# One more projection tile computed between the DeltaNet products, and the attention's mask product in rounded float32

## The chip, the cores and the metric

The kernel runs on one core of a Trainium2 chip. The metric is the time of one execution on the device, in microseconds (us). Before the change the median of three runs is 2902.16 us (2899.98 to 2906.4).

## The reference, cut to what matters

A two-layer decoder trunk over T = 1040 tokens (16 meta tokens, 1024 of input), model width 1024. Layer 0 has one input projection that feeds 4 gated-DeltaNet heads and 4 stick-breaking attention heads:

```python
proj = u @ w_in                      # 28 tiles of 128 columns, and the gates
q_a, k_a, v_a = silu(causal_depthwise_conv(qkv_a, conv_w))      # tiles 0 to 11; z_a: tiles 12 to 15
o_a = gated_delta_rule_chunked(q_a, k_a, v_a, g, beta)          # sequential over chunks
# stick-breaking attention, tiles q 16-19, k 20-23, v 24-27, per block of 128 queries:
z = einsum("bqhd,bkhd->bhqk", qb, k) * head_dim ** -0.5
causal = key_pos < query_pos                                    # strictly
log_w = log_sigmoid(z) + (sum_of_log_1m_after_key)
w = where(causal, exp(log_w), 0);  out = w @ v
```

Then an output projection, a SwiGLU feed-forward layer, an S5 state-space mixer with a GLU, and a second feed-forward layer. Nothing of these later stages is touched.

## The kernel before, in words

**Matrix products.** Large products are done in a split form. Every weight tile (slab, 128x1024) is loaded by SP's queue into `stage`, and POOL splits it into a rounded high part `w_hi` and a rest `w_lo` (type fp32r, "the rounded form"). `gemm` (L720 to L723) then issues three fp32r matmuls: high by high, high by low, low by high. A tile of the input projection is 3 column cuts of the tokens (352, 344, 344) by 8 slices of the inner dimension by 3 matmuls, so 72 matmuls. One slice of one cut, 3 matmuls, is called a *step*. Products outside `gemm` are plain f32, which shows as two MATMUL instructions for each product.

**Input projection.** `FIRST_FILLED` is 20. A loop of five iterations of four tiles each (L891) computes tiles 0 to 19. It writes PSUM banks in a ring of six: a tile in slot j uses banks (3j+c) mod 6, so tile 18 uses banks 0 to 2 and tile 19 banks 3 to 5. ACT moves each group out of its bank (`conv_tiles`, `plain_tiles` at L1475) and stores each tile to the DRAM tensor `proj` (L1451). Between tiles 17 and 18, ACT issues thirteen small stores of S5 tables (L1507 to L1516). Then PE transposes the gates' rows (L898), and `in_proj_steps(0, 24)` computes tile 20 in one piece into banks 0, 1 and 2, each group after the wait at L913, which asks that the bank's former group has been moved out.

**DeltaNet.** Nine blocks of 128 tokens (n = 0 to 8; the first is 16 tokens). Each block inverts a triangular matrix in up to six levels. A level is a product p (`dn_level_p`, L996 and L991), a copy by ACT (L1622), a product up (`dn_level_up`, L1017, L1021, L1025, L1013), and a subtraction and transposition by DVE (L2399, L2401). Behind or between them stand the products of the previous block's output (`dn_ks` L1034, `dn_vn` L1041, `dn_o` L1051 and L1052, `dn_kdv` L1059, `dn_o_turn` L1064) and of the next block's preparation. After each p and each up there is a *gap*. `fill(gap)` (L1077) puts two steps of the remaining projection tiles there, from gap 1 on. With seven tiles left (168 steps) gaps 1 to 84 are filled. Gap 84 is behind the first p of block 8, so the last 11 gaps, 85 to 95, are empty. All filled tiles except the first use one bank, `fill_bank`. ACT moves a finished group out at L1554 and stores a finished tile at L1558.

After block 8's levels come its own output products, called the tail below: `dn_ks(8)`, which waits for DVE's gated output of block 7 (L2440), then `dn_vn`, `dn_o`, `dn_kdv`, `dn_o_turn`. ACT, in the same stretch, waits for the stores of all 28 tiles and for block 7's gated output, issues the loads of attention heads 0 and 1 (`load_head`, L1705), and goes on to `dn_vn_sb(8)` (L1627).

**Attention.** 36 rounds (4 heads by 9 query blocks, `g`). PE transposes round g's weights (L1157), computes the scores of round g+2 (L1142), and multiplies round g's weights by the values (L1170). Where a score chunk crosses the diagonal, a mask product follows (L1145): the identity, 128x128, by a 128-column matrix of zeros and -1e30, added into the scores' bank. There are 11 of them for each head, 44 in all. Values are transposed at L1126.

## Time and profile before

| what | value |
|---|---|
| median of three runs | 2902.16 us (2899.98 to 2906.4) |
| the profiled execution's own time | 2906.43 us |
| its span | 2904.6 us |
| PE busy | 2763.2 us, 95% |
| PE weight load | 2631.2 us, 91% |
| DVE, ACT, POOL busy | 42%, 21%, 33% |
| mean granted clock of PE | 0.971 |
| input projection, after the gates | 60.4 to 302.4 us of the span |
| DeltaNet | 302.4 to 601.0 us |
| attention | 601.0 to about 741 us |

A duration of a matmul in the timeline reaches beyond the next one's start, since they overlap; what one costs in a stream is the distance between starts. The clock column is the granted TensorE clock as a share of 2.4 GHz: 1.00 or 0.50 (1.2 GHz), or a mean where it changes inside a window.

### The profile page before, as it was taken

Reading aid. Unit: us, or ns where it says so; the run is one execution under the profiler, and the core shown is the slowest. Engines: PE = TensorE matmul, PEld = TensorE weight load, DVE = VectorE, ACT = ScalarE, POOL = GpSimd, SP = SyncE. Lnnn points to the kernel's source line nnn. Section 1 sums busy time; section 2 is a strip of 40 time slices with the busy share of each in tenths; the row PEclk is TensorE's granted clock in tenths of the full one; section 3 lists DMA queues with packets and bytes.
Section 4 is the critical chain, followed back from the end, with each engine's and each line's share of the span. In section 5 each row is a group of like instructions: output and inputs, shape, how many; then the busy total and the mean of one; then the engine's idle time right before and its main releaser. Section 6 shows DMA issues by size and latency. Waiting matters only on the chain.

```text
span 2904.6 us, 45080 instructions
## 1 busy us (share of the span) xinstructions
PE 2763.2 (95%) x18337; PEld 2631.2 (91%) x18337; DVE 1229.3 (42%) x2118; ACT 616.3 (21%) x1079; POOL 969.0 (33%) x390
## 2 busy tenths in 40 slices
PE   8999899989999999999999977799999999999996
PEld 7999688867889999999999866699989999999996
DVE  4655565556053444444432535520443222222234
ACT  4221333346241000000000331320420000000012
POOL 4544111000343444444343313134424444434430
PEclk7999999989999999999999988899999999999998
DMA  4236312110231222222222238642221111111112
GB/s 139 88 104 127 92 60 78 34 67 23 84 103 56 79 82 84 87 81 81 81 82 82 77 102 231 207 126 59 95 95 44 43 51 51 43 43 43 44 30 78
DMA packets 156979, 236.48 MB, mean 81 GB/s; under 512 B 57664, under 2 KB 120384, under 8 KB 153664
## 3 DMA queue, kind: packets, MB, share of 16 engines
q1 hardware_dynamic: 52400, 137.11, 15.3%
q10 hardware_dynamic: 104464, 97.71, 11.1%
q8 instruction: 87, 1.43, 0.2%
q14 instruction: 28, 0.23, 0.0%
HBM read 174.89 MB, written 64.09 MB: 82 GB/s over the span
## 4 chain that ended last, share of the span: by engine, by line
PE 37%; issue 36%; POOL 14%; DMA 6%; DVE 3%; ACT 2%; ACTq 1%; POOLq 0%; SPq 0%; DVEq 0%
POOL w_hi L694 9%; PE psum L721 8%; PE psum L722 8%; PE psum L723 8%; POOL w_lo L697 5%; DMA stage<-wstream 4%; PE psum L781 2%; PE psum L1170 2%; PE psum L1142 1%; PE psum L996 1%; PE psum L1250 1%; DMA area<-s 1%; PE psum L1157 1%; PE psum L1017 1%; DVE area L2085 1%
## 5 line engine op out<-in xcount | busy, mean ns | idle before, releaser
L721 PE MATMUL psum<-x_hi,w_hi 128*128 128x344 f32 (+3 forms) x3600 | 1178.0, 327 | 29.0 <-DVE x_lo L2109 23.3
L722 PE MATMUL psum<-x_lo,w_hi 128*128 128x344 f32 (+3 forms) x3600 | 1160.8, 322 | 0.0
L723 PE MATMUL psum<-x_hi,w_lo 128*128 128x344 f32 (+3 forms) x3600 | 1159.0, 322 | 0.0
L694 POOL TENSOR_TENSOR w_hi<-stage,const 128x1024 fp32r<-128x1024 f32 x193 | 485.0, 2513 | 1836.6 <-PE psum L723 1807.2
L721 PEld LDWEIGHTS psum<-x_hi,w_hi 128*128 128x128 f32 x3600 | 687.6, 191 | 41.2 <-DVE x_lo L2109 21.6
L722 PEld LDWEIGHTS psum<-x_lo,w_hi 128*128 128x128 f32 x3600 | 687.6, 191 | 3.5 <-issue 1.7
L723 PEld LDWEIGHTS psum<-x_hi,w_lo 128*128 128x128 f32 x3600 | 686.8, 191 | 0.0
L697 POOL TENSOR_TENSOR w_lo<-stage,w_hi 128x1024 fp32r<-128x1024 f32 x193 | 488.2, 2530 | 15.1
L721 PE MATMUL psum<-act_hi,w_hi 128*128 128x344 f32 (+2 forms) x1056 | 343.6, 325 | 19.8 <-DVE area L2580 15.2
L2567 DVE TENSOR_TENSOR area<-area,psum 128x344 f32<-128x344 f32 (+2 forms) x132 | 67.7, 513 | 656.0 <-ACT area L1828 655.8
L723 PE MATMUL psum<-act_hi,w_lo 128*128 128x344 f32 (+2 forms) x1056 | 338.5, 321 | 0.0
L722 PE MATMUL psum<-act_lo,w_hi 128*128 128x344 f32 (+2 forms) x1056 | 337.6, 320 | 0.0
L2580 DVE TENSOR_TENSOR area<-area,psum 128x344 f32<-128x344 f32 (+2 forms) x480 | 243.2, 512 | 187.2 <-PE psum L723 184.8
L1828 ACT ACTIVATE area<-psum 128x344 f32<-128x344 f32 (+2 forms) x132 | 60.5, 458 | 1229.4 <-PE psum L723 1229.3
L721 PEld LDWEIGHTS psum<-act_hi,w_hi 128*128 128x128 f32 x1056 | 199.5, 189 | 24.8 <-DVE area L2580 19.3
L722 PEld LDWEIGHTS psum<-act_lo,w_hi 128*128 128x128 f32 x1056 | 201.4, 191 | 0.2
L723 PEld LDWEIGHTS psum<-act_hi,w_lo 128*128 128x128 f32 x1056 | 199.5, 189 | 0.0
L2176 DVE TENSOR_TENSOR area<-area 128x512 f32<-128x512 f32 (+7 forms) x282 | 164.5, 631 | 46.0 <-PE psum L1270 25.3
L2570 DVE TENSOR_TENSOR act_lo<-area,act_hi 128x344 fp32r<-128x344 f32 (+2 forms) x132 | 104.6, 792 | 77.9 <-ACT act_hi L1832 77.9
L781 PE MATMUL psum<-area,const 128*128 128x344 f32 (+2 forms) x384 | 117.1, 459 | 16.0 <-ACT area L1375 14.1
L781 PEld LDWEIGHTS psum<-area,const 128*128 128x128 f32 x384 | 72.7, 192 | 52.1 <-issue 14.0
L2085 DVE SCALAR_TENSOR_TENSOR area<-area,small,psum 128x344 f32<-128x344 f32 (+2 forms) x96 | 47.4, 566 | 105.8 <-ACT psum L1386 105.8
(226 smaller groups left out, 2053.3 us busy)
## 6 DMA issues: line engine op xcount, KB each, us to landing
stage<-wstream SPq DMA_DIRECT2D x193, 512.0 KB, 3.6
s_set<-area ACTq DMA_DIRECT2D x8, 1860.0 KB, 7.8
area<-s SPq DMA_DIRECT2D x8, 1348.0 KB, 9.2
proj<-area ACTq DMA_DIRECT2D x20, 520.0 KB, 2.7
area<-proj ACTq DMA_DIRECT2D x36, 256.0 KB, 4.1
resid<-area ACTq DMA_DIRECT2D x6, 1376.0 KB, 6.1
area<-resid ACTq DMA_DIRECT2D x6, 1376.0 KB, 8.4
area<-s SPq DMA_DIRECT2D x8, 1024.0 KB, 9.2
```

Source lines behind the costliest of these rows:

```text
L694: pool.tensor_tensor(per_block(w_hi[:, slot, :]), src, ones_block, ALU.mult).then_inc(high_split, 1)
L697: pool.tensor_tensor(per_block(w_lo[:, slot, :]), src, per_block(w_hi[:, slot, :]).bitcast(F32), ALU.subtract).then_inc(split_done, 1)
L721: mm(out[:, 0:n], w_hi[:, slot, wk], hi[:, xk, a:a + n], start=first, stop=False)
L722: mm(out[:, 0:n], w_hi[:, slot, wk], lo[:, xk, a:a + n], start=False, stop=False)
L723: return mm(out[:, 0:n], w_lo[:, slot, wk], hi[:, xk, a:a + n], start=False, stop=last)
L781: last = mm(sums[:, 0:n], ones, sq[k // 4][:, k % 4, 0:n], start=(k == 0), stop=(k == KT - 1))
L1828: A(gate[st % 2][:, 0:n], bank[2 * (st % 2)][:, 0:n], ACT.Silu).then_inc(silu_done, 1)
L2085: last = V.scalar_tensor_tensor(out=acc[:, k, a:a + n], in0=acc[:, k, a:a + n], scalar=small[:, at:at + 1], in1=rr, op0=mul, op1=mul)
L2176: tt = lambda o, a, b, op: ch(V.tensor_tensor(o, a, b, op))
L2567: V.tensor_tensor(f[st % 2][:, 0:n], gate[st % 2][:, 0:n], bank[2 * (st % 2) + 1][:, 0:n], mul).then_inc(act_f32, 1)
L2570: V.tensor_tensor(act_lo[:, st % 2, a:a + n], f[st % 2][:, 0:n], act_hi[:, st % 2, a:a + n].bitcast(F32), sub).then_inc(act_ready, 1)
L2580: last = V.tensor_copy(o, src) if first else V.tensor_tensor(o, o, src, add)
```

## The change

`FIRST_FILLED` becomes 19. The loop runs four iterations, tiles 16, 17 and 18 follow it unrolled, and tile 19, the scaled query tile of head 3, is the first filled one: it is computed in one piece by `in_proj_steps(0, 24)` into banks 0, 1 and 2, which tile 18 used just before. Eight tiles are then left for the gaps (192 steps), so gaps 1 to 95 are filled and the last two steps stand in front of the tail. ACT evacuates the last group there, scales tile 19 in `filled_evac`, and asks for the last tiles' stores only before it loads head 2. The mask product takes both operands from `w_hi`, as fp32r, in a part of slot 5 that is free there; DVE writes them with one more copy.

```diff
-FIRST_FILLED = 20
+FIRST_FILLED = 19
...
+        mask_weights, mask_values = (w_hi[:, 5, 512 + P * i:512 + P * i + P] for i in range(2))
...
             with pe.Fori(0, FIRST_FILLED // 4) as i:
                 tile_groups("in_proj", i, 6)
+            tile_groups("in_proj", FIRST_FILLED // 4, 6, count=FIRST_FILLED % 4)
...
-                        pe.wait_ge(group_free, g + 1 if tile == 0 else 6 + g)
+                        pe.wait_ge(group_free, g + 4 if tile == 0 else 6 + g)
...
             o = BLOCKS - 1
+            in_proj_steps((N_PROJ - FIRST_FILLED) * 3 * KT - FILL_STEPS, FILL_STEPS)
             dn_ks(o)
...
-                        last = mm(z[0:nq, d - a:m], ident[:, 0:nq], sv["neg"][:, d - q0:a + m - q0], start=False, stop=True)
+                        last = mm(z[0:nq, d - a:m], mask_weights[:, 0:nq], mask_values[:, d - q0:a + m - q0], start=False, stop=True)
...
-            plain_tiles(SQ + 2, ACT.Copy, HD ** -0.5)
+            plain_tiles(SQ + 2, ACT.Copy, HD ** -0.5, 1)
...
             def load_head(hd):
+                if hd == 2:
+                    for i in range(2):
+                        act.wait_ge(proj_stored[i], 16 * (1 + N_PROJ // 2))
...
+            filled_evac(3 * (N_PROJ - FIRST_FILLED) - 1)
             for i in range(2):
-                act.wait_ge(proj_stored[i], 16 * (1 + N_PROJ // 2))
+                act.wait_ge(proj_stored[i], 16 * (1 + SV // 2 + 1))
             act.wait_ge(dn["o_gated"], BLOCKS - 1)
             load_head(0)
             load_head(1)
...
-            V.tensor_scalar(sb_views(carve)["neg"], incl, -1e30, None, mul).then_inc(sk["neg"], 1)
+            V.tensor_copy(mask_weights, ident)
+            V.tensor_scalar(mask_values, incl, -1e30, None, mul).then_inc(sk["neg"], 1)
```

## Rows read from the trace of the kernel before

**Rows 1.** The page, busy time and share of the span of each engine.
```profile
PE 2763.2 (95%) x18337; PEld 2631.2 (91%) x18337; DVE 1229.3 (42%) x2118; ACT 616.3 (21%) x1079; POOL 969.0 (33%) x390
```

**Rows 2.** Timeline of ACT, end of the projection: start, length, instruction, [idle before <-releaser].
```profile
289.57 0.63 ACTq L1516 DMA_DIRECT2D s_tab<-area  x1
290.30 1.16 ACT L1475 ACTIVATE area<-psum 128x352 f32<-128x352 f32 x3 [23.32 <-PE psum L723]
```

**Rows 3.** Timeline of PE, from the end of the projection loop to DeltaNet's first product.
```profile
289.24 0.77 PE L898 MATMUL psum<-const,area 64*128 64x64 f32 x9
290.91 0.40 PE L721 MATMUL psum<-x_hi,w_hi 128*128 128x352 f32 x1 [0.90 <-ACT area L1475]
...
303.79 1.10 PE L935 MATMUL psum<-area,const 128*128 128x512 f32 x2 [1.27 <-ACT area L1579]
```

**Rows 4.** Windows: length, busy of PE, PEld, DVE, ACT, POOL, PEclk, DMA share, GB/s.
```profile
45.00:60.00 15.00, 15.00 (x73) 15.00 (x71) 1.10 (x4) 5.00 (x12) 6.69 (x3) 0.50 0.40 145
277.80:289.10 11.30, 11.30 (x73) 11.22 (x71) 0.00 (x0) 0.00 (x0) 4.79 (x2) 1.00 1.37 147
1700.50:1703.00 2.50, 2.50 (x9) 2.50 (x10) 0.00 (x0) 0.00 (x0) 0.00 (x0) 0.50 0.00 0
1703.50:1706.00 2.50, 2.50 (x18) 2.50 (x18) 0.00 (x0) 0.24 (x1) 0.00 (x0) 1.00 0.00 0
2141.00:2146.50 5.50, 5.50 (x19) 5.50 (x20) 0.86 (x2) 0.49 (x1) 0.00 (x0) 0.50 0.00 0
```

**Rows 5.** Timeline of PE, where the window at 1700 us begins.
```profile
1700.37 0.65 PE L721 MATMUL psum<-x_hi,w_hi 128*128 128x344 f32 x1 [7.23 <-DVE x_lo L2109]
```

**Rows 6.** Timeline of PE, block 7 of DeltaNet, filled gap behind an up and an output product.
```profile
541.67 0.68 PE L1017 MATMUL psum<-area 64*64 64x64 f32 x16
542.29 1.16 PE L1034 MATMUL psum<-area 128*128 128x128 f32 x8
...
544.34 0.68 PE L996 MATMUL psum<-area 64*64 64x64 f32 x16
```

**Rows 7.** Timeline of PE, block 8: one filled gap, then empty ones, and the tail.
```profile
566.33 0.68 PE L996 MATMUL psum<-area 64*64 64x64 f32 x16
...
568.08 0.68 PE L1017 MATMUL psum<-area 64*64 64x64 f32 x16
569.28 0.68 PE L996 MATMUL psum<-area 64*64 64x64 f32 x16 [0.52 <-DVE area L2399]
570.45 0.68 PE L1017 MATMUL psum<-area 64*64 64x64 f32 x16 [0.48 <-ACT area L1622]
571.06 1.16 PE L1034 MATMUL psum<-area 128*128 128x128 f32 x8
572.15 0.68 PE L996 MATMUL psum<-area 64*64 64x64 f32 x16
...
583.85 1.11 PE L1064 MATMUL psum<-const,area 128*128 128x128 f32 x4
586.02 2.05 PE L1034 MATMUL psum<-area 128*128 128x128 f32 x8 [1.06 <-DVE dn_result L2440]
...
600.98 2.25 PE L1126 MATMUL psum<-const,area 128*128 128x128 f32 x9 [0.97 <-DVE dn_result L2440]
```

**Rows 8.** Timeline of ACT, between block 7's gated output and the tail.
```profile
585.98 2.81 ACTq L1705 DMA_DIRECT2D area<-proj  x6
```

**Rows 9.** Windows of the tail, the attention's opening, and the attention.
```profile
584.00:597.00 13.00, 10.47 (x44) 9.31 (x44) 1.76 (x4) 2.11 (x11) 0.00 (x0) 0.50 0.65 246
601.00:614.00 13.00, 13.00 (x46) 9.39 (x46) 4.18 (x11) 6.51 (x17) 0.00 (x0) 0.50 0.00 1
640.00:726.00 86.00, 83.07 (x524) 64.06 (x524) 54.00 (x75) 51.43 (x121) 0.00 (x0) 1.00 0.06 19
```

**Rows 10.** Timeline of PE in the attention, a mask product and what follows it.
```profile
644.43 0.39 PE L1145 MATMUL psum<-area,const 128*128 128x128 f32 x2
644.65 0.80 PE L1170 MATMUL psum<-area 128*128 128x128 f32 x4
```

More of the change, by code:

```diff
@@ L261, in sb_views @@
     v["vt"] = [carve(at + BLOCKS * P * i, BLOCKS * P) for i in range(2)]
-    v["neg"] = carve(at + 2 * BLOCKS * P, P)
     return v
@@ L723, in gemm, with tile_groups @@
                 return mm(out[:, 0:n], w_lo[:, slot, wk], hi[:, xk, a:a + n], start=False, stop=last)
-            def tile_groups(name, i, group0, cuts=CUTS, x_from=None):
+            def tile_groups(name, i, group0, cuts=CUTS, x_from=None, count=SLOTS):
                 _, slots = slots_of(name)
-                for j, slot in enumerate(slots):
+                for j, slot in enumerate(slots[0:count]):
                     pe.wait_ge(split_done, split_value(name, i, j))
@@ L1466, in conv_tiles, with plain_tiles @@
                     proj_store(u, s)
-            def plain_tiles(first, func, scale=1.0):
-                for u in (first, first + 1):
+            def plain_tiles(first, func, scale=1.0, count=2):
+                for u in range(first, first + count):
                     i, s = divmod(u, 4)
@@ L1525, in _ @@
             for i in range(2):
-                act.wait_ge(proj_stored[i], 16 * (1 + FIRST_FILLED // 2))
+                act.wait_ge(proj_stored[i], 16 * (1 + (FIRST_FILLED + 1 - i) // 2))
             act.wait_ge(s5["tab_stored"], 16 * 13)
@@ L1553, in filled_evac @@
                 act.wait_ge(group_done, g + 1)
-                A(filled_out[u % 2][:, a:a + n], (bank[c] if tile == 0 else fill_bank)[:, 0:n], ACT.Copy
-                  ).then_inc(group_free, 1)
+                A(filled_out[u % 2][:, a:a + n], (bank[c] if tile == 0 else fill_bank)[:, 0:n], ACT.Copy,
+                  scale=HD ** -0.5 if u < SK else 1.0).then_inc(group_free, 1)
                 if c == len(CUTS) - 1:
```

## The prediction

> **What bounds the kernel now.** I read the page first: PE is busy 95% of the span [rows 1], so a change pays only where it takes PE time away or fills a hole of PE, and where nothing else then ends last. The change touches three places, so I read each one's timeline. At the end of the projection the thing to see is ACT, not PE: ACT is in its queue issuing small stores until 290.2 us, and only then moves tile 18 out of banks 0 to 2 [rows 2]. PE had finished tile 18 long before; it had gone on to tile 19 in other banks, and stands 0.90 us for that evacuation before the first filled tile [rows 3]. In block 8 of DeltaNet, each level without filler shows PE waiting about half a microsecond for ACT after p and for DVE after up [rows 7]. In the windows the granted clock is the thing to see: 0.50 in the tail of DeltaNet and in the attention's opening, 1.00 in the rest of the attention, where PE is busy 83.07 of 86 us [rows 9].
>
> **The tile that leaves the loop.** It is 72 matmuls at 11.30 / 72 = 0.157 us, 11.3 us of PE time [rows 4]. In the new order tile 18 ends at about 277.8, and the transposes (0.77 us) move up behind it. But tile 19 now goes into banks 0 to 2, and its wait counts to the same number as before: old g = 66 with g + 1 is 67, new g = 63 with g + 4 is 67. That is the evacuation of tile 18's first group, and ACT gets to it at 290.30, behind the table stores, which PE's pace does not touch [rows 2]. So the first filled tile starts at 290.9 as before, and the 11.3 us become a hole of 12.3 us. The gain of this part is nothing.
>
> The hole has a price. After 7.23 us without work, PE restarts at 1700.37 [rows 5] at the clock 0.50, and is at 1.00 by 1703; at 2141 it stays low for 5.5 us of dense matmuls [rows 4]. Low, one matmul takes 5.50 / 19 = 0.289 us, so a microsecond at the low clock loses 1 - 0.157 / 0.289 = 0.46 us. I take a loss of 1.9 us, between 2.6 x 0.46 = 1.2 and 5.5 x 0.46 = 2.5. The tile used to end at 303.79 - 1.27 = 302.5, and DeltaNet's first product waited for ACT's squares until 303.79 [rows 3]. ACT has one evacuation and one store less ahead of those squares, so they come sooner. The tile now ends at 304.4 and is what ends last: **+0.6 us** (-1.3 if the clock doesn't fall, +1.2 with the longer recovery).
>
> **Filler in block 8.** Gaps 85 to 95 and the two steps ahead of the tail take 24 steps, the same 72 matmuls. A bare gap, with nothing else between two products, goes from 1.17 to 1.20 us between starts when empty to 1.75 when filled (566.33 to 568.08 against 568.08 to 569.28 and 569.28 to 570.45) [rows 7]: +0.57 each, for gaps 85, 86, 88, 93 and 94, in all 2.9. A gap beside an output product has no wait to hide in: up, `ks`, filler, p takes 2.67 us in block 7 [rows 6], and 1.70 without filler in block 8 [rows 7]: +0.97 each for gaps 87, 89, 90, 91 and 92, in all 4.8; I take off 0.5, since 90 and 92 hold a short wait for ACT. Gap 95 and the last two steps stand between L1064 and L1034, which are 2.17 us apart through the wait for DVE's gated output [rows 7]. The four steps need 12 x 0.157 = 1.9 us and L1064 itself about 0.6, so 2.5: +0.4. The sum is **+7.6 us** (7.0 to 9; the whole price of 72 matmuls without cover is 11.3). ACT's evacuations in the block fall where they did in the earlier blocks, and hide. POOL's split that waits for tile 25 comes one block later, still far ahead of the output projection, which wants it: nothing.
>
> **The tail.** Before, PE's clock is 0.50 through it: 10.47 us of PE work in 584 to 597 [rows 9], of which 0.9 is L1064. The same eight matmuls take 1.16 us at 571.06 and 2.05 at 586.02 [rows 7]. The last filler ended at 568.1, and the clock fell behind 571 and ahead of 584. Now the last filler stands directly ahead of the tail, and filled block 7 shows L1034 at 1.16 us too, the full clock [rows 6]. So I take the tail at 2.4 GHz: 9.5 us become 9.5 x 1.16 / 2.05 = 5.4, -4.1. Against it stands ACT. It must move the last group out, store it, and issue six loads, 2.81 us [rows 8], before it can copy `vn`; PE and DVE now have `vn` ready after two products of 1.16 and a DVE step between, some 3.1 us, and ACT is free at 2.81 plus about 0.9 for the group and its store: +0.6. Together **-3.5 us** (0 if the clock falls at once, -5 if the value transposes L1126 run fast as well). The six loads have 12 us instead of 15 before they are wanted; head 0's come first, so nothing. DVE's extra copy is hidden by L1126.
>
> **The mask products.** A pair of f32 instructions occupies PE 644.65 - 644.43 = 0.22 us [rows 10]. In rounded form there is one instruction. The nearest row is the gates' stage, fp32r matmuls of 172 columns, at least 15.00 / 73 = 0.205 us each at the clock 0.50 [rows 4], so about 0.11 at full clock, and 128 columns can't be slower. I take 0.11, half the pair. Of 11 for each head, two stand in front of a product that waits for ACT anyway (the small one of query block 0, and block 1's), so 36 of 44 count: 4.0 us, and five in the attention's opening save twice as much at the low clock, 0.5 more: **-4.5 us** (0 if a change of type costs PE as much, -7 if a product costs only its columns, 0.06). The attention is bound by PE [rows 9], so little of it is lost.
>
> The Trainium skill (FP8 and Floating Point Precision, "TensorE Precision Notes") says that a true float32 product takes four passes of the array and the reduced form reads the value truncated. By that rule a mask product would fall to a quarter, and 36 of them would save about 6 us instead of 4; the sum would be about 2901. No row of the kernel before shows so narrow an fp32r product; the nearest, the gates' above, speaks for a floor.
>
> **The attention's opening.** 13 us at 0.50 with PE busy throughout [rows 9]. The end of the tail is as thin in PE work as before, so I expect the clock to fall there and the opening to be as slow: 0 (-5 if it stays up: 13 x 0.46 is 6, less the waits for ACT and DVE that would appear).
>
> **Sum.** 0.6 + 7.6 - 3.5 - 4.5 = +0.2 us on the profiled execution's own time of 2906.43. That execution lies 4.3 us above the median of the runs, 2902.16, so the forecast for the median is 2902.4.
>
> **Rivals.**
> The clock holds into the attention. For it: the tail starts from a dense stretch. Against it: its last 4 us, 597 to 600.98, have little but one group of transposes, and the opening behind them was low from its first microsecond [rows 7, 9]. Then +0.2 - 5 = -4.8: 2897.6.
> The clock falls in the tail after all: for it, its chain of PE, DVE and ACT leaves PE idle for a fifth of the time even at the low clock [rows 9], and for more at the high one. The filler's cost is not given back: +0.2 + 3.5 - 0.6 (ACT's delay is hidden again) = +3.1: 2905.5.
> The masks gain nothing, because going from f32 to fp32r and back costs what the second instruction did. For it: the distance behind a first fp32r matmul after f32 ones is longer; against it: the same shows after narrow fp32r ones. +4.7: 2907.1. With the one before, 2910.2.
> The slower side: the first filled tile runs cold to its end. PE was busy for all of 45 to 60 us and its clock stayed at 0.50 [rows 4]. Then the tile takes 72 x 0.289 = 20.8 us instead of 11.3, ends at 312, and DeltaNet starts 8.2 us late: 0.2 - 0.6 + 8.2 = +7.8, 2910.2. It is slower by more than 0.2% when the low clock lasts longer than about 16 us. Against it: those were other matmuls, the gates'; both restarts with the very matmuls of this tile recovered.
> The hole doesn't form: ACT reaches tile 18 sooner. Then 0.2 - 0.6 - 11.3 = -11.7, 2890.7. Against it: the stores stand on ACT's own queue, in the 23.32 us between two of its evacuations [rows 2], and wait for nothing of PE.
>
> **How the numbers follow.** The forecast has 0.48, its own range is 2899 to 2906. The clock holding has 0.12, the tail low 0.14, the masks without gain 0.12 (0.03 of it with the tail low), the cold tile 0.08, no hole 0.06. A measurement of this kernel tells 0.2%, 5.8 us, from no change. Faster by more: no hole, a part of the clock holding, and masks at their best, 0.18. Slower by more: the cold tile, two failures together, and some spread, 0.17. The rest, 0.65, is the same. The range for 8 of 10 is 2896.5 to 2909: it leaves out the missing hole and the cold tile.
>
> **What would show it.** Right: PE idle from about 278.6 to 290.9 with the clock low after it; L935 at about 304.4; gap 86 at 1.75 us; L1034 of the tail at about 594 with 1.1 us, not 2; half the MATMUL instructions on L1145, 0.11 us apart from the next. Wrong: the first filled tile starting before 290; block 8 lengthened by under 6 or over 9 us; the tail's clock at 0.50; a head of the attention no shorter than before.

## The result and the profile after

The changed kernel took 2914.2 us (2906.05 to 2916.38, 6 runs), the kernel before 2904.28 in the same session (2899.98 to 2910.87, 6 runs): ratio 1.0027, 95% interval 1.0014 to 1.004. It is 7.8 us slower (4.1 to 11.6), where no change had been forecast. Two more measurements of the same kernel gave 1.0026 (1.0015 to 1.0036) and 1.0017 (1.0007 to 1.0027), so 5 to 8 us. The forecast had been 2902.4 us, within 2896.5 to 2909.

The page has hardly moved. PE does 10 us less work than in [rows 1], and has 44 instructions fewer, the second halves of the mask products.

```profile
PE 2753.0 (95%) x18293; PEld 2622.0 (90%) x18293; DVE 1234.9 (42%) x2119; ACT 616.4 (21%) x1079; POOL 967.8 (33%) x390
```

The end of the projection: timeline of ACT, to be read beside [rows 2].

```profile
269.90 0.34 ACTq L1453 DMA_DIRECT2D proj<-area  x1
270.27 3.92 ACTq L1509 DMA_DIRECT2D s_tab<-area  x4
274.22 10.64 ACTq L1513 DMA_DIRECT2D s_tab<-area  x6
...
288.84 3.10 ACTq L1518 DMA_DIRECT2D s_tab<-area  x1
292.04 1.16 ACT L1477 ACTIVATE area<-psum 128x352 f32<-128x352 f32 x3 [22.18 <-issue]
```

PE at the same place, beside [rows 3].

```profile
280.70 0.77 PE L899 MATMUL psum<-const,area 64*128 64x64 f32 x9
292.65 0.63 PE L721 MATMUL psum<-x_hi,w_hi 128*128 128x352 f32 x1 [11.18 <-ACT area L1477]
...
305.92 1.02 PE L936 MATMUL psum<-area,const 128*128 128x512 f32 x2
```

ACT is inside its own queue from 270.3 to 292.0, thirteen small stores. PE, a tile ahead of where it was, stands 11.18 us for the same evacuation as before. In the other seven profiles that have this hole it is 12.2 to 13.8 us. (This execution started its projection 2.7 us later than the profiled one of before, so 292.65 answers to 289.9.) The windows show the clock: 0.50 in the hole, 0.54 behind it, where the first filled tile lies.

```profile
284.00:292.00 8.00, 0.00 (x0) 0.00 (x0) 0.00 (x0) 0.00 (x0) 1.61 (x1) 0.50 1.36 130
292.00:297.00 5.00, 4.35 (x16) 4.38 (x17) 0.00 (x0) 2.44 (x4) 0.00 (x0) 0.54 0.56 167
```

Block 8, with filler in each gap, beside [rows 7]: 1.77 us from a p product to the next up product in a bare gap (577.99 to 579.76), 2.63 from up to the next p in a gap that holds an output product too (579.76 to 582.39).

```profile
577.99 0.68 PE L997 MATMUL psum<-area 64*64 64x64 f32 x16
579.76 0.68 PE L1018 MATMUL psum<-area 64*64 64x64 f32 x16
580.37 1.16 PE L1042 MATMUL psum<-area 128*128 128x128 f32 x8
582.39 0.68 PE L997 MATMUL psum<-area 64*64 64x64 f32 x16
```

The tail, beside [rows 7, 8]: ACT, then PE.

```profile
597.44 0.46 ACT L1556 ACTIVATE spare_slots<-psum 128x344 f32<-128x344 f32 x1 [3.83 <-PE psum L723]
597.92 0.36 ACTq L1560 DMA_DIRECT2D proj<-spare_slots  x1
598.40 3.28 ACTq L1710 DMA_DIRECT2D area<-proj  x6
601.73 0.60 ACT L1629 ACTIVATE area<-psum 128x512 f32<-128x512 f32 x1 [3.84 <-DMA proj<-spare_slots]
```

```profile
597.24 1.05 PE L1035 MATMUL psum<-area 128*128 128x128 f32 x8
599.07 1.16 PE L1042 MATMUL psum<-area 128*128 128x128 f32 x8 [0.78 <-DVE area L2423]
602.38 0.49 PE L1052 MATMUL psum<-area 128*128 128x128 f32 x2 [2.15 <-ACT area L1629]
...
603.60 0.40 PE L1053 MATMUL psum<-area 128*128 128x128 f32 x2
603.82 0.61 PE L1052 MATMUL psum<-area 128*128 128x128 f32 x2
604.23 0.63 PE L1053 MATMUL psum<-area 128*128 128x128 f32 x2
604.65 1.91 PE L1060 MATMUL psum<-area 128*128 128x128 f32 x8
...
610.45 1.81 PE L1128 MATMUL psum<-const,area 128*128 128x128 f32 x8 [0.97 <-DVE dn_result L2446]
```

The tail starts fast, as forecast (L1035 takes 1.05 us, against 2.05 before). Then PE stands 2.15 us for the copy L1629, which stands behind six load issues on ACT, and from 603.8 on the granted clock is low: a pair of products takes 0.6 instead of 0.4 us.

A mask product with the whole of its round, from the round's transposes to the next round's:

```profile
649.76 0.44 PE L1159 MATMUL psum<-const,area 128*128 128x128 f32 x2
650.04 0.84 PE L1144 MATMUL psum<-area 128*128 128x400 f32 x2
650.41 0.53 PE L1147 MATMUL psum<-w_hi 128*128 128x128 f32 x1
650.78 0.86 PE L1172 MATMUL psum<-area 128*128 128x128 f32 x4
651.57 0.55 PE L1159 MATMUL psum<-const,area 128*128 128x128 f32 x3
```

The same round in the kernel before, around [rows 10]:

```profile
643.48 0.44 PE L1157 MATMUL psum<-const,area 128*128 128x128 f32 x2
643.75 0.84 PE L1142 MATMUL psum<-area 128*128 128x400 f32 x2
645.38 0.55 PE L1157 MATMUL psum<-const,area 128*128 128x128 f32 x3
```

One row would mislead here. From the mask product to the next product it is now 0.37 us, more than the 0.22 of the f32 pair; but from the scores' product to the mask it is 0.37 where it was 0.68. The round is 1.81 us long against 1.90, and that is the gain.

To compare, I cut each profile into stages by the starts of PE's products. The first 60.4 to 63.4 us, ahead of the projection, are the same work in every kernel and are left out. The front runs from the projection's first product to `ks(0)` of DeltaNet, the blocks end with `ks(8)`, the tail with the attention's first value transpose. Means over profiles, in us:

```
                           before (3)   after (3)   difference
front: to the transposes     228.96      218.15       -10.8
       to DeltaNet's start    13.79       25.96       +12.2
       to ks(0)               42.43       42.47         0.0
blocks, to ks(8)             241.42      249.17        +7.75
tail                          14.80       13.24        -1.6
head 0                        21.25       21.11        -0.1
heads 1 to 3, to w_out       114.60      111.15        -3.45
w_out to the last step      2140.8      2144.9        (+4.1)
```

The last line has the same instructions in both kernels. Between the three executions of the kernel before alone it runs from 2135.2 to 2145.5, so three profiles of each can't tell whether any of its 4.1 us comes with the change; I leave it out of the account. (Cut by the count of instructions into 24 pieces, this stretch agrees within 0.2 us in 17 of them over all twenty profiles. What scatters sits in seven pieces, and two of these hold the restarts at the low clock of [rows 4, 5].) The front scatters too. The eight profiles with the hole taken in all have a mean of 287.5 (285.0 to 289.6) there, the four of kernels with the tile in the loop and ACT's stores where they were 285.2 (284.1 to 286.9): +2.4. With that, the account is 2.4 + 7.75 - 1.6 - 0.1 - 3.45 = +5.0 us. It lies inside all three intervals, near the lower end of two.

### The profile page after: what moved, and what is told of

It reads as the page before. It is cut to its first block, busy times and chain, and to the rows that moved or that the text cites. A ratio compares the mean times of both kernels' runs of the same rounds, so it can differ in the third digit from the quotient of the medians.

```text
span 2907.6 us, 44980 instructions
## 1 busy us (share of the span) xinstructions
PE 2753.0 (95%) x18293; PEld 2622.0 (90%) x18293; DVE 1234.9 (42%) x2119; ACT 616.4 (21%) x1079; POOL 967.8 (33%) x390
## 4 chain that ended last, share of the span: by engine, by line
PE 37%; issue 36%; POOL 14%; DMA 6%; DVE 4%; ACT 2%; ACTq 1%; POOLq 0%; SPq 0%; DVEq 0%
POOL w_hi L694 9%; PE psum L721 8%; PE psum L722 8%; PE psum L723 8%; POOL w_lo L697 5%; DMA stage<-wstream 4%; PE psum L781 2%; PE psum L1172 2%; PE psum L1144 1%; PE psum L997 1%; DMA area<-s 1%; PE psum L1252 1%; PE psum L1018 1%; PE psum L1159 1%; DVE area L2091 1%
```

## The experiments

Differences between two kernels timed together, with a 95% interval, are worked out from the times of their runs (means). Ratios to the kernel before can be compared safely only between kernels timed together: on one chip it took 2906.8 us in one session and 2915.9 in a later one.

### The change again, and its parts

The changed kernel, unaltered:

> The changed kernel itself once more, for its executions' spread and a second profile. Its first profile (span 2907.6, clock 0.974) has the whole account at +0.5 us against the kernel before once both are counted from the gates on, while four of its six executions lie at 2914 to 2916 with the clock at 0.970. Theory H (the hole): PE stands idle for 11.2 us before the first filled tile, and how long the low clock lasts behind it differs from one execution to the next; expects a profile of a 2914 execution to show the extra 7 to 8 us between 292 and 345 us of the span. Theory M (masks): the attention's opening stays at the low clock longer in those executions; expects the extra in 600 to 640. Theory S (start): it lies in the first 65 us, loads and gates, and would come to the kernel before as well; expects then a ratio near 1.001.

Measured: 2912.44 us, ratio 1.0026 (1.0015 to 1.0036). The result stands, and theory S's 1.001 lies outside. Against the first profile the front is 2.8 us longer and head 0 is 3.0, the tail 0.8 shorter: neither H nor M has its 7 to 8 us in one place.

The kernel before with the rounded mask alone:

```diff
-    v["neg"] = carve(at + 2 * BLOCKS * P, P)
+        mask_weights, mask_values = (w_hi[:, 5, 512 + P * i:512 + P * i + P] for i in range(2))
-  last = mm(z[0:nq, d - a:m], ident[:, 0:nq], sv["neg"][:, d - q0:a + m - q0], start=False, stop=True)
+  last = mm(z[0:nq, d - a:m], mask_weights[:, 0:nq], mask_values[:, d - q0:a + m - q0], start=False, stop=True)
...
+            V.tensor_copy(mask_weights, ident)
```

> The kernel before with the mask product in rounded form and nothing else. H: the masks are a plain gain, 1.04 us for each later head as the first profile of the changed kernel shows and about 3 for the first: 2898, -5 to -6 against before. M: no faster than before, or slower, with the opening's clock at 0.50 for longer than 14 us. S: -5 to -6 as well.

Measured: 2903.23 us, ratio 0.9994 (0.9983 to 1.0004). That is no faster than before beyond its interval, and less than the 5 to 6 us expected. By the stages each later head is 31.01 us long against 32.05, and the last stretch to the output projection 49.13 against 50.50. Round by round within a later head, the seven rounds whose scores need a mask that counts are shorter by 0.10 to 0.16 us, or by 0.22 where there are two masks; the other two, in front of ACT's waits, by nothing. That makes the nine products of 11 that the prediction let count.

The changed kernel with the mask product in f32 as before, the other way round:

> The changed kernel with the mask product in plain float32 again: tile 19 as first filled tile, filler through block 8. H: slower than the changed kernel by 5 to 6, so 2919, +14 against before, with the executions spread as widely as its. M: +6 to +8 against before with little spread. S: +6 to +8 (0.7 in front, 7.6 in block 8, -1.8 in the tail).

Measured: 2917.75 us, ratio 1.0045 (1.0029 to 1.0061), 5.3 us (3.6 to 7.2) above the changed kernel timed with it. So the masks are worth 3.5 us in the stages and 3.6 to 7.2 by the times, and the slow-down is the tile's. The kernel with the mask alone is 8.8 us (6.6 to 11.1) below the changed one: that is the tile's price as the change moved it.

### The hole

The changed kernel with 72 more matmuls, whose result nobody reads, while PE would wait:

```diff
+            pe.wait_ge(group_free, 6 + 6 + 3 * 17 + 3)
+            for k in range(3 * KT):
+                gemm(bank[3], 3, k % KT, k % KT, CUTS[1], k % KT == 0, k % KT == KT - 1)
```

> The changed kernel with 72 more matmuls of the projection's kind (tile 19's weights, results thrown away in bank 3) on PE in the hole, between the gates' transposes and tile 19. Output unchanged. They end at about 292, where tile 19 could start anyway. H: the clock stays at 1.00, tile 19 and DeltaNet's block 0 run as in the kernel before, and the spread goes: 2905 to 2907, 7 to 9 below the changed kernel's median. M and S: at most 1 to 2 us faster than the changed kernel (1.9 us of low clock taken away), so 2912.

Measured: 2910.78 us, ratio 1.002 (1.0008 to 1.0031), 1.6 us below the changed kernel (from 3.7 below to 0.6 above). So the hole's low clock is not the whole of the slow-down: theory H had wanted 7 to 9. Windows of it, the hole and what follows: the clock never falls.

```profile
281.00:292.00 11.00, 11.00 (x75) 10.72 (x75) 0.00 (x0) 0.00 (x0) 4.77 (x2) 1.00 1.31 161
292.00:297.00 5.00, 3.90 (x25) 3.65 (x24) 0.00 (x0) 2.45 (x4) 0.00 (x0) 1.00 0.80 127
```

In the eight profiles with an empty hole, the filled tile's matmuls start over 12.6 to 13.9 us from first to last, against 11.3 in the four with the tile in the loop; the mean is 1.8 longer. That is the clock's part of the hole, and the times alone, with zero inside the interval, would not have told it. The front of this kernel is 285.8 us.

Two kernels of before, for its scatter, and one with ACT's thirteen stores issued by SP between two weight loads:

```diff
+                elif name == "in_proj":
+                    with sp.Fori(0, 5) as i:
+                        load(i)
+                    store_tables()
+                    with sp.Fori(5, count) as i:
+                        load(i)
```

> The kernel before once more, for a second profile. The tail of DeltaNet (from ks(8) to the first value transposes) took 14.96 us in its first profile, at the clock 0.50, and 10.58 us in mask_only, which has the same code there and no filler in block 8, at 1.00. Theory T: the tail's clock in the kernel before is a matter of the execution, so what the filler was credited with is mostly not its own; expects 10.5 to 15 here, whichever. Theory F (as predicted: the filler keeps the clock up): 15 again.

> The kernel before a third time. T: of the three profiles at least one has the tail at 10.6 to 11. F: 15 in all. For the front (start of the projection to DeltaNet's first product) both expect 243.4 as before, and from there to ks(0) 40.7 to 41.8.

> The changed kernel with the thirteen S5 table stores issued by SP's queue, between the weight loads of tiles 19 and 20, instead of by ACT. If ACT's stores are what holds tile 18's evacuation, the hole goes: the first filled tile starts within 1 us of the transposes, at about 281, at full clock. But ACT's loads for DeltaNet still wait until the tables have landed, so its first product stays near 303 (both theories); total 1 to 3 below the changed kernel. If something else holds bank 0, PE still waits some 11 us.

Measured: 2898.75, 2905.42 and 2902.97 us, one time each, too few to compare kernels by. The tails of the two profiles of before are 14.96 and 14.49 us, so theory T's fast tail without filler did not come in them. With the stores off ACT's queue there is no hole: the filled tile follows the transposes at once. DeltaNet then starts 234.9 us after the projection's first product, where it was 242.8 and had been expected to stay. But from the start of DeltaNet to `ks(0)` it took 46.3 us instead of 42.4.

### The tail

The copy `dn_vn_sb(8)` ahead of the last filled evacuation and of the loads:

```diff
+            dn_vn_sb(BLOCKS - 1)
             filled_evac(3 * (N_PROJ - FIRST_FILLED) - 1)
...
             load_head(0)
             load_head(1)
-            dn_vn_sb(BLOCKS - 1)
```

> The changed kernel, ACT copying vn of block 8 before it evacuates the last filled group, stores it and issues the six loads. The tail took 13.2, 12.4, 14.1 and 12.6 us in the four kernels with filler through block 8, against 10.58 without. T: the 2 us are ACT's queue (0.6 was predicted); expects a tail of 11.0 to 11.3 in this profile if its clock is up, and 1 to 2 us off the median: ratio 1.002. F: the tail is slower because of the clock; no change.

Measured: 2911.4 us, ratio 1.0015 (1.0004 to 1.0027), tail 13.42 us, not shorter at all. PE's wait for the copy is down to 0.69 us, and the products behind it run at the full clock. But ACT's timeline shows what came instead: the six issues, 3.80 us, now stand ahead of the next thing that PE and DVE want of ACT.

```profile
603.02 0.60 ACT L1629 ACTIVATE area<-psum 128x512 f32<-128x512 f32 x1 [6.66 <-PE psum L1042]
...
604.47 3.80 ACTq L1710 DMA_DIRECT2D area<-proj  x6
608.32 0.28 ACT L1636 ACTIVATE area<-psum 128x128 f32<-128x128 f32 x1 [4.36 <-DMA proj<-spare_slots]
```

PE waits 4.63 us there, at `dn_o_turn`, where it waits 2.25 in the changed kernel, and its clock is low behind that wait. So the issues had to leave ACT. Four kernels timed together: the loads of heads 0 and 1 on SP ahead of the output projection's weights; the tables on SP, with only block 1's loads waiting for them; both; and both without the tile's move.

```diff
+                elif name == "w_out_a":
...
+                    for hd in range(2):
+                        for m, x in ((SV, "v"), (SQ, "q"), (SK, "k")):
+                            sp.dma_start(sv[x][hd % 2], proj[m + hd][:, FRONT:T_ROWS]).then_inc(sk[f"loaded{hd % 2}"], 16)
+                    for i in range(count):
+                        load(i)
```

> The changed kernel with the six loads of heads 0 and 1 issued by SyncE, ahead of the out-projection's weights, instead of by ScalarE, which issues them between the last filled evacuation and dn_vn_sb(8). Theory (the filler kept the clock up in the tail as forecast, and ScalarE's issue of the loads took back the gain): from ks(8) to the first product with the values 10.6 to 11.2 us, as without filler at full clock (10.58), against 12.4 to 14.1 in four profiles of kernels with the filler; the copy L1629 starts right after the last filled group's evacuation, near 598 to 599 us; total about 2.3 us below the changed kernel. Rival (the tail is late for another reason, such as the tensor engine's clock or the DMA traffic): 12.4 to 14.1 us again and the same total. Head 0 stays at 19 to 22 us in either case.

> The changed kernel with the thirteen table stores of the S5 part issued by SyncE between two weight loads, and with only the second block's loads (dn_load(1), its z, its zeroed u) waiting for them, so that DeltaNet's block 0 can start as soon as the tile before it is stored. Theory (the hole ahead of the first filled tile and the late start are both ScalarE's 22 us of store issue): no idle over 2 us ahead of the first filled tile, DeltaNet's first sum at 288 to 291 us instead of 305.9 in the changed kernel and 302 to 303 in the one before; from the in-projection's start to ks(0) 274 to 281 us against 285 before and 287 after; ratio to the kernel before 0.995 to 0.998. Rival (the opening of DeltaNet is slow at a low clock once the engine has drained, so that the time is given back): ks(0) no earlier than with the stores alone moved (282), ratio 0.999 to 1.001.

> Both moves together: tables and the loads of heads 0 and 1 from SyncE, the tile out of the loop, filler through block 8, rounded mask. If the two are independent: the kernel with the moved tables less 2.3 us, ratio to the kernel before 0.994 to 0.997. If the late start of the projection's last weight loads (they wait behind the stores in SyncE's queue) costs something, the first filled tiles wait for weights and the ratio is above 0.998.

> The kernel before (tile 19 in the loop, no filler in block 8) with the rounded mask and both moves. It tells what the tile's move is worth once ScalarE is out of its way. Theory (the tile costs 7.9 us in block 8 wherever it is taken from, and its removal from the loop is worth its 11.4 us only if DeltaNet can start that much earlier): this kernel keeps the early part 8 to 11 us longer than the one with both moves and the tile moved, saves 7.9 in block 8, and the two totals lie within 3 us, ratio to the kernel before 0.996 to 0.999. Rival (moving the tile costs more than it gives even so): this kernel is the fastest of the four, by over 3 us.

Measured: 2915.01 (ratio 1.0023, 1.0013 to 1.0032), 2905.97 (0.9989, 0.9978 to 1.0), 2909.57 (1.0004, 0.9994 to 1.0014) and 2914.52 us (1.0018, 1.0008 to 1.0028). All four missed what was expected of their ratios: both moves together are slower than the tables alone, and the kernel without the tile's move is neither within 3 us of the one with it nor the fastest. The loads' kernel has the forecast tail, 10.50 us, and gives all of it back: head 0 takes 27.14 us. DVE's timeline in it, then POOL's:

```profile
614.25 2.23 DVE L2544 TENSOR_TENSOR_SCAN area<-area 128x144 f32<-128x144 f32 x1 [0.46 <-ACT area L1745]
616.51 2.26 DVE L2547 TENSOR_TENSOR area<-area 128x143 f32<-128x143 f32 x1
```

```profile
613.82 2.35 POOL L704 TENSOR_TENSOR w_hi<-stage,const 128x1024 fp32r<-128x1024 f32 x1 [133.24 <-DMA stage<-wstream]
616.24 2.37 POOL L707 TENSOR_TENSOR w_lo<-stage,w_hi 128x1024 fp32r<-128x1024 f32 x1
```

Each of these DVE instructions, which read and write SBUF alone, ends 0.2 to 0.3 us after the POOL instruction beside it: a scan of 144 columns takes 2.23 us instead of the 0.46 in a kernel with no split there (the last one below). The weights of the output projection wait in SP's queue behind the head loads, which wait for DeltaNet, so POOL splits them now; in the changed kernel the last split ahead of the attention begins at 538.95, in the middle of DeltaNet. The tables' kernel has the same at the front, where DeltaNet starts at 297.3 us (288 to 291 had been expected). Its four splits of tiles 20 to 23 run from 292.7 to 314.4 us, on DeltaNet's opening, and a copy of 128x4 takes as long as one of them:

```profile
309.71 2.31 DVE L2369 COPY area<-area 128x4 f32<-128x4 f32 x1
311.94 1.11 DVE L2370 TENSOR_SCALAR area<-psum,area 128x128 f32<-128x128 f32 x4
312.97 2.00 DVE L2377 TENSOR_TENSOR area<-area 128x512 f32<-128x512 f32 x1
```

The Trainium skill (SBUF — State Buffer, "SBUF: two separate sides") says that a GpSimd instruction shares one pair of SBUF ports with a VectorE instruction that is in a two-port mode or, where the GpSimd one reads SBUF, has two SBUF inputs; whichever starts first holds the pair for its whole length, and the other fully blocks. This case's traces agree: the split at 309.46 starts ahead of the copy at 309.71, and the copy takes 2.31 us here and 0.16 in the kernel with both moves below; the four operations from PSUM at 311.94 run beside a split at their usual 0.28 each. No run moved the splits alone; that they cost the opening and head 0 their time is shown by the next four kernels, in which the issues moved together with them.

### Both issues off ACT, and clear of the splits

The same moves, later in SP's queue: the head loads behind the first four weight loads of the output projection, the tables behind those of tiles 20 to 23.

```diff
-                elif name == "w_out_a":
+                elif name == "w_out_b":
+                    load(0, js=range(0, 2))
...
+                    load(0, js=range(2, SLOTS))
...
-                    with sp.Fori(0, 5) as i:
+                    with sp.Fori(0, 6) as i:
                         load(i)
                     store_tables()
-                    with sp.Fori(5, count) as i:
-                        load(i)
+                    load(6)
```

> As the kernel that had SyncE issue the loads of heads 0 and 1, but behind the first four weight loads of the out-projection, which go out early, as in the changed kernel, instead of ahead of them. So GpSimd splits no weights in head 0. Theory (head 0's 27.2 us were VectorE's scans beside GpSimd's splits: a 128x144 scan took 2.23 us there against 0.46): tail 10.5 us as there, head 0 back at 19 to 22 us, total 2 to 2.5 us below the changed kernel, ratio to the kernel before 1.0015 to 1.0025. Rival (head 0 was late because the tail had come early, by the clock): tail and head 0 together 36 to 38 us as there, ratio 1.002 to 1.003 and head 0 above 24 us.

> As the kernel with the S5 tables stored by SyncE, but four weight loads later in SyncE's queue, behind those of tiles 20 to 23. There the splits of these four ran at 292.7 to 314.4 us, on top of DeltaNet's opening, and a VectorE copy of 128x4 took 2.31 us. Here at most one split (of tile 23) is left, at about 292 to 297 us. Theory (collision): DeltaNet's first sum near 297 us as there, and from it to ks(0) 40 to 43 us instead of 45.6; ratio to the kernel before 0.997 to 0.998. Rival (the clock is low because the tensor engine drained, splits or not): 45 to 47 us again, ratio 0.9985 to 1.

> Both moves in their later places. If the two collisions are gone and the two gains independent: 2.5 us below the kernel with the tables alone moved, ratio to the kernel before 0.996 to 0.9975, the best of all. If the gain of the tail comes back as a low clock in head 0, the same total as with the tables alone.

> The kernel before (tile 19 in the loop, no filler in block 8) with the rounded mask and the tables stored by SyncE, behind the weight loads of tiles 20 to 23. It tells the tile's own price by comparison with the kernel that has the tile moved and the tables stored so. Theory: the tile gives at most 11.4 us at the front and costs 7.9 in block 8 and 2.5 in the tail (14.1 against 10.6 without filler), so the two are within 2 us of each other, ratio to the kernel before 0.9965 to 0.999. Rival (DeltaNet can't start earlier than the stored tile can be loaded back, so that moving the tile gives far less than 11.4): this kernel is faster than the other by 3 us or more.

Measured, with the stages of each profile:

```
                  us       ratio (95%)               front   blocks  tail   head 0
loads_sp2       2913.61   0.9990 (0.9979 to 1.0001)  289.6   249.2   10.5   17.6
tables_sp2      2909.18   0.9970 (0.9959 to 0.9981)  281.6   249.2   12.5   22.1
both_sp2        2906.04   0.9963 (0.9950 to 0.9976)  280.9   249.2   10.5   21.5
mask_tables_sp2 2913.11   0.9992 (0.9982 to 1.0003)  291.8   241.7   14.9   21.2
```

The timeline of PE in `both_sp2`, with both moves: the tile follows the transposes, ends at 291.85, and DeltaNet starts 6.66 us later.

```profile
291.54 0.31 PE L757 MATMUL psum<-x_hi,w_lo 128*128 128x344 f32 x1
298.51 2.05 PE L970 MATMUL psum<-area,const 128*128 128x512 f32 x2 [6.66 <-ACT area L1596]
```

And its DVE in the opening: the copy that had taken 2.31.

```profile
310.93 0.16 DVE L2373 COPY area<-area 128x4 f32<-128x4 f32 x1
311.00 1.12 DVE L2374 TENSOR_SCALAR area<-psum,area 128x128 f32<-128x128 f32 x4
```

Both collisions are gone (head 0 takes 17.6 to 22.1 us, where the three kernels with the early head loads had 23.1 to 27.1), and from DeltaNet's start to `ks(0)` it is 42.7 to 42.9 instead of 45.6. DeltaNet starts later than with the earlier stores, though (at 302.0 against 297.3 with the tables alone), as its first loads now run beside the stores: ACT's timeline of the tables' kernel has 8.61 us of wait for a DMA there, where the one with the earlier stores had 4.01. (That the stores slow these loads is read from the overlap, not shown by a run.)

```profile
290.75 1.55 ACTq L1545 DMA_DIRECT2D area<-proj  x3
...
301.22 1.15 ACT L1586 ACTIVATE area<-area 128x512 f32<-128x512 f32 x2 [8.61 <-DMA area<-proj]
```

The kernel with both moves is faster than the kernel before by 0.37% (0.24 to 0.50), and its interval lies clear of all three of the changed kernel. So does that of the tables alone, which it betters by 1.6 us, with an interval from 0.7 above to 3.8 below, where 2.5 had been expected. The loads' kernel came out 0.25 to 0.35% faster against the kernel before than expected. The stages say less than the ratio: against the kernel before -4.3 us at the front, +7.75 in the blocks, -4.3 in the tail and -3.45 in the later heads, together -4.3, where the ratio gives -10.8. That the kernel before stood high at that time may be in it; that the new one is faster is shown, not by how much. And of the -4.3 the rounded masks, which need none of this, are 3.45: by the stages the tile with both moves is worth 0.9 us. The last kernel had been expected within 2 us of the one with the tile moved; it is 5.8 us (3.5 to 8.2) slower. With the stores on SP the tile's move pays: it gives 10.2 us at the front, takes 7.5 in block 8, and gives 2.4 in the tail. But those 10.2 are counted from a kernel whose front the late stores had made longer themselves, 291.8 us where `mask_only`, with the stores on ACT, has 285.1. Against `mask_only` the tables' kernel gains 3.5 at the front, less than block 8 costs.

The changed kernel and the one with the head loads moved, on one chip, since two sessions had put them 10 us apart where the tail accounts for 2.7:

> The changed kernel once more, beside the kernel with the moved head loads on the same chip. If the change costs the same everywhere: ratio to the kernel before 1.0015 to 1.0035. If it was the chip: 1.000 to 1.0015.

> The changed kernel with the loads of heads 0 and 1 issued by SyncE behind the first four out-projection weight loads, once more. By the stages (tail 10.5 us against 12.4 to 14.1, nothing else touched) it is 2 to 3 us below the changed kernel on the same chip, 0.0007 to 0.001 in the ratio. If the move is worth what the two chips suggested, it is 8 us or more below it.

Measured: 2914.76 us (ratio 1.0017, 1.0007 to 1.0027) and 2908.13 (0.9994, 0.9983 to 1.0005); the second is 7.0 us (4.2 to 10.0) below the first. The tail is 10.50 us against 14.10, 3.6 of the 7. ACT now waits 2.37 us for PE ahead of its copy, PE waits only 0.69 for the copy, and the clock holds through the tail:

```profile
600.27 0.60 ACT L1639 ACTIVATE area<-psum 128x512 f32<-128x512 f32 x1 [2.37 <-PE psum L1052]
```

```profile
600.92 0.49 PE L1062 MATMUL psum<-area 128*128 128x128 f32 x2 [0.69 <-ACT area L1639]
...
602.81 1.06 PE L1070 MATMUL psum<-area 128*128 128x128 f32 x8
```

The difference is more than the stage shows, less than the two chips had suggested; where the rest of it lies (0.6 to 6.4 us) stays open. The front and the later heads don't have it, head 0 has 0.8 of it, and the part behind w_out was 2.5 us longer in the faster kernel's profile.

## Why the prediction failed

The places were the right ones, three of four mechanisms too; three terms were too kind, by 1.8, 1.9 and 1.0 us. Summed again with the measured terms: +5.0 instead of +0.2. That is the part of the miss that the stages show. The forecast of 2902.4 lies 11.8 us under the measured median: 2.1 of them are the kernel before, whose median went from 2902.16 with three runs to 2904.28 with six, 4.8 are these terms, and the other 4.9 stay open. The interval of the change, 4.1 to 11.6, allows them to be scatter, and the stretch behind w_out may hold some.

Every sign that the prediction named for being right came, but for one (the 0.11 us from a mask product to the next), and of those for being wrong only the tail's low clock, in a part of the tail: the signs tested where the time would go, not the sizes that decide a sum near nothing.

**The hole**: right. PE idle 11.18 us where the prediction had 12.3, the start set by ACT's stores, the clock low behind it. **Its price**: +0.6 was forecast, +2.4 measured. The loss of 1.9 us to the clock was right (1.8 by the tile's length). The credit against it was not: DeltaNet's first product had waited 1.27 us in the one execution profiled, and the step took all of it as gained. In three more profiles with the tile in the loop the gap behind the tile's last matmul says 0.1 to 0.5 us; the mean over four is 0.6. The other 1.2 us are 0.8 in when the first filled tile can start, relative to the projection's start (231.6 against 230.8, scatter 229.6 to 232.8), and some 0.4 in the opening; both are within what executions differ by.

**Block 8**: +7.6 forecast, +7.75 measured; a bare gap 1.77 us (1.75 forecast), one with a product 2.63 (2.67).

**The tail**: the failed step. -3.5 was forecast, -1.6 measured. That the filler lets the tail start at full clock, and what that is worth, was right: 14.96 - 4.1 = 10.9 forecast, 10.50 measured in all five profiles with the filler and without the loads on ACT. (Without filler it was 14.3 to 15.0 in five profiles and 10.58 in one, the mask's; so the clock can hold there without filler too, but seldom.) The step went wrong at "ACT is free at 2.81 plus about 0.9 for the group and its store: +0.6". `vn` was ready 3.0 us after `ks(8)` began, as forecast (3.1), but ACT was free only at 4.4, not 3.7: the issues took 3.28 us, and group and store 1.2. PE waited 2.15 us instead of 0.69, which is 1.5; and behind the wait PE went on at a lower clock, which is the other 1.2 (means over three profiles). All eight profiles with the filler and the loads' issue ahead of the copy have this wait, 1.4 to 1.6 us longer, and in all eight the clock falls before the tail is over, in some at once and in some only at `dn_o_turn`; their tails are 12.3 to 14.1 us. In the five with the same loads issued by SP at nearly the same time it holds, so it is ACT's time and not the transfers. A wait in a thin stretch was priced at its length alone. The same block of ACT issue, moved by one instruction, cost the same in another place.

**The masks**: -4.5 forecast. In the later heads the step was right: 9 products at 0.11 are 1.0, 1.04 measured, and the rounds that gain are the ones it named; the last stretch gave 1.37. Head 0 was to give 1.5 and shows 0.1, under a scatter of 3 us between executions that its low clock makes: by the times the masks are worth 5.3 (3.6 to 7.2), so this term is not refuted. The Trainium skill's four passes (FP8 and Floating Point Precision, "TensorE Precision Notes") would have made it, as an estimate, 1.5 us for each head (9 x 0.165); no head shows that. (With that rule the prediction's sum would have been 2900.4, not 2901.) What holds the narrow rounded product at half the f32 pair was not tested.

**The rivals.** The clock did not hold into the attention. The masks gained. The cold tile didn't come: the tile took 12.6 to 13.9 us, not 20.8. The tail's rival (+3.1) was nearest, and half true: its clock fell on the way, behind the wait for ACT, where the same thin work without that wait kept it. No rival put two blocks of DMA issue on ACT as one cause, though both rows [rows 2, 8] had been read: 22 and 3 us of an engine that PE waits for. The range ended at 2909, 5 us short, since each of these terms had been bounded around one execution's rows.

## What to carry to other kernels

Count a block of DMA issues as busy time of the engine that issues it, at every place where another engine waits for that engine next; moving the wait past it by one instruction only chooses who pays. Moving the issue to a free queue pays, if the loads queued behind it are not pushed onto another engine's critical time: follow each of them to its consumer. And a credit of about 1 us, taken from one wait in one execution, wants a second execution before it is counted; what a wait costs includes the clock that falls in it.

## What the runs showed of the hardware

- A DVE copy, scan or tensor_tensor with all operands in SBUF stood for a whole POOL tensor_tensor that had begun before it: 2.31 us for a copy of 128x4 (0.16 alone), 2.23 for a scan of 128x144 (0.46 alone); head 0 took 27.1 us instead of 21. DVE instructions with an input in PSUM did not (0.28 each, as usual).
- Thirteen strided stores cost ACT 21.7 us of issue, and SP 25.6 (273.8 to 299.4 with both moves) or 19.0 (265.5 to 284.5 with the earlier place); the six loads of two heads' tiles cost 2.8 to 3.8 us on ACT and 2.8 to 3.0 on SP.
- With a single wait of 2.1 to 2.3 us in the tail the granted clock fell to 0.50 behind it in eight profiles of eight, 1.4 us after the wait's end in the changed kernel's first profile, at once in another, in others 5 us later, around the next wait of 2.25 us. With 0.69 instead, and the same 2.25 behind it, it held in five of five.
- Giving the mask products in fp32r instead of f32 saved 1.04 us a head, 0.10 to 0.16 of the pair's 0.22 in each round with one mask that counts, 0.11 in most: half, not three quarters.
- The same kernel on the same chip took 2906.8 us in one session and 2915.9 in a later one. In all twenty profiles the dense stretches behind w_out are alike within 0.2 us; the scatter, up to 14 us there, lies in the few stretches that hold restarts.
